# Attention and retention contractions of 16, 64 and 1 rows brought to 128 rows, and the chunk mask moved into maxima and exponentials

## What is computed

```python
q = (rms_norm(c_q, cq_g) @ w_uq).reshape(bn, lp, 16, 128 + 64)       # latent attention, 16 heads
s = einsum(q_nope, k_nope) + einsum(q_rope, k_rope)                  # k_rope is shared by all heads
mask = valid[None, :] & (cid[None, :] <= qcid[:, None])              # cid = position // 64
p = softmax(where(mask, s * MLA_SCALE, -1e30))
o_a = einsum('bhqk,bkhd->bqhd', p, v)
# retention, 8 heads of 256, chunkwise: scores * decay, times values, plus a carried state
s = einsum('bnhd,bmhd->bhnm', qc, kc) * intra
o_b = silu(g) * groupnorm(s @ vc + (qc @ state) * xi)
merged = sigmoid(ga) * (o_a @ w_pa) + sigmoid(gb) * (o_b @ w_pb)
h = layer_norm(ALPHA * h + merged @ w_out)
h = layer_norm(ALPHA * h + moe(h))                                   # 32 experts, top 2 of one group
```

## Time and profile before

| | |
|---|---|
| median of three runs | 2192.99 us (2190.24 to 2193.17) |
| profiled execution | 2191.38 us, of which the span from first to last instruction is 2189.6 us |
| PE busy | 2096.2 us, 96% |
| DVE busy | 1579.4 us, 72% |
| ACT busy | 1262.1 us, 58% |
| DMA, mean share of 16 engines | 40 to 60% until 1100 us, full from 1200 us |
| mean granted TensorE clock | 0.986 |

### The profile page before, as it was taken

The page is one execution under the profiler, slowest core; times in us unless marked ns, Lnnn a source line. Parts: engine busy times, 40 slices in busy tenths (PEclk is TensorE's granted clock), DMA queues, the critical chain, the costliest instruction groups (busy, mean ns, idle before and its releaser), DMA issues.

```text
span 2189.6 us, 30203 instructions
## 1 busy us (share of the span) xinstructions
PE 2096.2 (96%) x11524; PEld 1756.2 (80%) x11524; DVE 1579.4 (72%) x1373; ACT 1262.1 (58%) x1004; POOL 107.4 (5%) x78
## 2 busy tenths in 40 slices
PE   7999999999999999999999999999999999999991
PEld 6998777899999997887787778777877777777771
DVE  6645444453545455445668999999999999999996
ACT  5434433333232323333346888888888888888881
POOL 1000000000000000000000000000000000000000
PEclk9999999999999999999999999999999999999995
DMA  6554234655454544556865999999999999999993
GB/s 206 144 145 157 97 108 144 213 175 183 143 173 140 174 146 141 187 192 226 251 242 212 414 421 420 422 420 420 419 419 417 420 419 416 418 415 419 418 370 137
DMA packets 164615, 602.40 MB, mean 275 GB/s; under 512 B 20336, under 2 KB 28672, under 8 KB 113440
## 3 DMA queue, kind: packets, MB, share of 16 engines
q1 hardware_dynamic: 160800, 593.81, 71.5%
q0 software_dynamic: 3744, 7.59, 1.1%
HBM read 595.05 MB, written 18.89 MB: 280 GB/s over the span
## 4 chain that ended last, share of the span: by engine, by line
PE 69%; DVE 14%; DMA 7%; issue 7%; ACT 2%; POOL 0%; DVEq 0%; POOLq 0%; SPq 0%; ACTq 0%
PE ps L1720 20%; PE ps L1704 14%; DVE wl L667 11%; DMA raw<-in_w_dram 7%; PE ps L953 6%; PE ps L954 5%; PE ps L2075 4%; PE ps L950 3%; ACT wh L543 2%; PE ps L1825 2%; PE ps L1805 2%; PE ps L975 2%; PE ps L923 1%; PE ps L1792 1%; DVE yall L801 1%
## 5 line engine op out<-in xcount | busy, mean ns | idle before, releaser
L667 DVE TENSOR_TENSOR wl<-raw,wh 128x2048 fp32r<-128x2048 f32 x352 | 792.6, 2288 | 39.8 <-ACT wh L543 38.5
L543 ACT ACTIVATE wh<-raw 128x2048 fp32r<-128x2048 f32 x352 | 671.3, 1915 | 134.0 <-DMA raw<-in_w_dram 81.9
L1329 DVE TENSOR_TENSOR wl<-raw,wh 128x2048 fp32r<-128x2048 f32 (+1 forms) x169 | 382.1, 2264 | 290.1 <-ACT wh L1145 290.0
L1145 ACT ACTIVATE wh<-raw 128x2048 fp32r<-128x2048 f32 (+1 forms) x169 | 320.0, 1896 | 454.7 <-DMA raw<-in_w_in_dram 278.1
L953 PE MATMUL ps<-wh,xg 128*128 128x512 f32 x900 | 374.8, 416 | 21.4 <-DVE wl L667 21.3
L954 PE MATMUL ps<-wl,xg 128*128 128x512 f32 x900 | 352.9, 392 | 0.0
L1704 PE MATMUL ps<-hth,wh 128*128 128x272 f32 (+1 forms) x896 | 260.1, 290 | 3.2 <-DVE wl L1329 1.8
L1704 PE MATMUL ps<-htl,wh 128*128 128x272 f32 (+1 forms) x896 | 257.2, 287 | 0.0
L1704 PE MATMUL ps<-hth,wl 128*128 128x272 f32 (+1 forms) x896 | 256.9, 287 | 0.0
L953 PEld LDWEIGHTS ps<-wh,xg 128*128 128x128 f32 x900 | 169.8, 189 | 72.7 <-DVE wl L667 32.6
L953 PE MATMUL ps<-wh,hx 128*128 128x512 f32 x508 | 202.9, 399 | 4.2 <-DVE hx L794 4.2
(11 more groups left out here) (340 smaller groups left out, 3074.3 us busy)
## 6 DMA issues: line engine op xcount, KB each, us to landing
raw<-in_w_dram SPq DMA_DIRECT2D x384, 1024.0 KB, 10.3
raw<-in_w_in_dram SPq DMA_DIRECT2D x104, 1024.0 KB, 5.1
raw<-in_w_pa_dram SPq DMA_DIRECT2D x16, 1024.0 KB, 5.1
raw<-in_w_pb_dram SPq DMA_DIRECT2D x16, 1024.0 KB, 5.1
raw<-in_w_out_dram SPq DMA_DIRECT2D x16, 1024.0 KB, 5.2
raw<-in_w_ukv_dram SPq DMA_DIRECT2D x8, 1024.0 KB, 5.4
yrow<-yscr SPq DMA_DIRECT2D x4, 1024.0 KB, 8.1
raw<-in_w_uq_dram SPq DMA_DIRECT2D x8, 384.0 KB, 3.5
```

The source lines that it names most:

```text
L543: nc.scalar.activation(wh2[:, x % HELD, :], raw2[:, slot2(x), :], ACT.Copy).then_inc(s_wh2, 1)
L667: nc.vector.tensor_tensor(wl2[:, slot2(x), :], raw2[:, slot2(x), :], wh2[:, x % HELD, :].bitcast(F32), ALU.subtract).then_inc(s_wl2, 1)
L1145: nc.scalar.activation(wh[:, n % RING1, 0:c], raw1[:, n % RING1, 0:c], ACT.Copy).then_inc(s_wh, 1)
L1329: nc.vector.tensor_tensor(wl[:, n % RING1, 0:c], raw1[:, n % RING1, 0:c], wh[:, n % RING1, 0:c].bitcast(F32), ALU.subtract).then_inc(s_wl, 1)
```

## The change

Every small contraction now spans 128 rows:

- `vm`, `ptm`, `vnm` and `stm` are declared with 128 partitions. Their rows 16 to 127 are set to zero once and stay zero; the copies still write the first 16 rows.
- `kr` has two planes of 128 rows. Plane a holds the rotary key in the half of its rows that belongs to head a of a pair, and zeros in the other half. The product takes all 128 rows of the queries of both heads of the pair.
- The mask product is gone. The maxima and exponentials run over the keys that a half tile of 64 queries sees (`SEEN`: 80, 144, 208 and 272 keys): four instructions on 64 partitions in place of two on 128, on DVE and on ACT. The masked places of `prob` are set to zero once.
- The query latents are computed for 256 columns in place of 272, and the operations on them are narrower by as much.
- DVE zeroes `kr` after its setup copies and `ptm`, `prob` and `vm` after the `lo` of the next unit; `vnm` and `stm` are zeroed after the attention loop, with a semaphore `s_zero` on which ACT waits before retention.
- The table `rowmask`, its DMA and the two small ACT copies of it and of the ones are gone, and some constants lie elsewhere.

```diff
@@ -32,7 +32,7 @@
-LAT_BANK, SS_BANK = (0, 4), (6, 5)
+LAT_BANK, SS_BANK, LAT_C0 = (0, 4), (6, 5), (N_META, 0)
@@ -132,15 +132,17 @@
-        vm = place("vm", [N_META, H_MLA * VH], A0 + 17408)
+        vm = place("vm", [P, H_MLA * VH], A0 + 17408)
+        SEEN = [(t, slice(64 * c, 64 * (c + 1)), KT0 * t, KT0 * t + (KT0, KT1)[t] - 64 * (1 - c))
+                for t in range(TT) for c in range(2)]
-        ptm = place("ptm", [N_META, 2, SEQ], 199680)
+        ptm = place("ptm", [P, 2, SEQ], 199680)
-        vnm = place("vnm", [N_META, 2 * DK], R0 + 4096)
+        vnm = place("vnm", [P, 2 * DK], R0 + 4096)
-        stm = place("stm", [N_META, 2, SEQ], R0 + 9216)
+        stm = place("stm", [P, 2, SEQ], R0 + 9216)
-        kr = place("kr", [P, LT], K0 + 4736)
-        rowmask = place("rowmask", [1, P], K0 + 5824)
+        kr = place("kr", [P, 2, LT], K0 + 3712)
...
@@ -1184,10 +1186,10 @@
-                for t, (c0, c1) in enumerate(((0, KT0), (KT0, KT0 + KT1))):
-                    e = nc.scalar.activation(prob[:, h % 2, c0:c1], ps[:, 4 + h % 2, c0:c1], ACT.Exp,
-                                             bias=amax[:, h % 2, t:t + 1], scale=MLA_SCALE,
-                                             accum_out=asum[:, h % 2, t:t + 1])
+                for t, r, c0, c1 in SEEN:
+                    e = nc.scalar.activation(prob[r, h % 2, c0:c1], ps[r, 4 + h % 2, c0:c1], ACT.Exp,
+                                             bias=amax[r, h % 2, t:t + 1], scale=MLA_SCALE,
+                                             accum_out=asum[r, h % 2, t:t + 1])
...
@@ -1236,9 +1238,6 @@
-                if n == 2:
-                    nc.scalar.activation(rowmask_r[:, :], rowmask[:, :], ACT.Copy)
-                    nc.scalar.activation(ones_r[0:1, 0:64], ones[0:1, 0:64], ACT.Copy).then_inc(s_msk, 1)
@@ -1255,6 +1254,7 @@
+            act.wait_ge(s_zero, 1)
...
-                nc.vector.tensor_tensor(kr[:, :], krt[:, :], krt2[:, :], ALU.add).then_inc(s_kr, 1)
+                for a in range(2):
+                    r = slice(ROPE * a, ROPE * (a + 1))
+                    k = nc.vector.tensor_tensor(kr[r, a, :], krt[r, :], krt2[r, :], ALU.add)
+                k.then_inc(s_kr, 1)
...
-                nc.vector.tensor_reduce(amax[:, h % 2, 0:1], ps[:, 4 + h % 2, 0:KT0], AXX, ALU.max)
-                own.after(nc.vector.tensor_reduce(amax[:, h % 2, 1:2], ps[:, 4 + h % 2, KT0:KT0 + KT1], AXX, ALU.max))
+                for t, r, c0, c1 in SEEN:
+                    m = nc.vector.tensor_reduce(amax[r, h % 2, t:t + 1], ps[r, 4 + h % 2, c0:c1], AXX, ALU.max)
+                own.after(m)
...
+                    nc.vector.memset(kr[:, :, :], 0.0)
+                if n == 3:
+                    nc.vector.memset(ptm[:, :, :], 0.0)
+                    nc.vector.memset(prob[:, :, :], 0.0)
+                    own.after(nc.vector.memset(vm[:, :], 0.0))
...
+            nc.vector.memset(vnm[:, :], 0.0)
+            nc.vector.memset(stm[:, :, :], 0.0).then_inc(s_zero, 1)
...
             for u in range(4):
-                t_unit(N_CQ + u, 0, u, [(b, 0, True) for b in range(4)])
+                t_unit(N_CQ + u, 0, u, [(b, X0, True) for b in range(4)], c0=X0, width=SEQ)
...
@@ -1843,11 +1857,7 @@
-                    nc.tensor.matmul(o, qro[ROPE * a:ROPE * (a + 1), 2 * g, q], kr[ROPE * a:ROPE * (a + 1), 0:kt],
-                                     start=False, stop=False, skip_group_check=True)
-
-                    m = nc.tensor.matmul(ps[:, 4 + h % 2, c0 + kt - 64:c0 + kt], rowmask_r[:, :], ones_r[0:1, 0:64],
-                                         start=False, stop=True, skip_group_check=True)
+                    m = nc.tensor.matmul(o, qro[:, 2 * g, q], kr[:, a, 0:kt], start=False, stop=True, skip_group_check=True)
```

More of the change, by code:

```diff
@@ L168, in moe_trunk @@
         ones = place("ones", [P, P], K0 + 1024)
-        cos_b = place("cos_b", [P, LT], K0 + 2560)
-        sin_b = place("sin_b", [P, LT], K0 + 3648)
-        kr = place("kr", [P, LT], K0 + 4736)
-        rowmask = place("rowmask", [1, P], K0 + 5824)
-        rowmask_r = place("rowmask_r", [1, P], K0 + 5824, F32R)
-        ones_r = place("ones_r", [1, 64], 203904, F32R)
+        cos_b = place("cos_b", [P, LT], K0 + 1536)
+        sin_b = place("sin_b", [P, LT], K0 + 2624)
+        kr = place("kr", [P, 2, LT], K0 + 3712)
         lngb = place("lngb", [P, 2, KD], K0 + 6336)
@@ L200, in moe_trunk @@
         s_x = [sem(f"s_x{t}") for t in range(TT + 1)]
-        s_msk = sem("s_msk")
+        s_zero = sem("s_zero")
         s_raw = [sem(f"s_raw{i}") for i in range(RING1)]
@@ L1197, in transposed @@
                 nc.scalar.activation(pt[:, h % 2, :], ps[:, 4 + h % 2, 0:3 * P], ACT.Copy)
-                nc.scalar.activation(ptm[:, h % 2, :], ps[0:N_META, 6 + h % 2, SEQ:2 * SEQ],
+                nc.scalar.activation(ptm[0:N_META, h % 2, :], ps[0:N_META, 6 + h % 2, SEQ:2 * SEQ],
                                      ACT.Copy).then_inc(s_ptc, 1)
@@ L1264, in values @@
                 else:
-                    nc.scalar.activation(vnm[:, :], ps[0:N_META, 6, :], ACT.Copy).then_inc(s_vn, 1)
+                    nc.scalar.activation(vnm[0:N_META, :], ps[0:N_META, 6, :], ACT.Copy).then_inc(s_vn, 1)
             def ret_gate(g):
@@ L1379, in scale_latents @@
                 dve.wait_ge(s_sq, count)
-                own.after(nc.vector.reciprocal(crs[:, j, :], crs[:, j, :]))
+                c = LAT_C0[j]
+                own.after(nc.vector.reciprocal(crs[:, j, c:LT], crs[:, j, c:LT]))
                 for b in range(KR):
-                    nc.vector.scalar_tensor_tensor(csq[:, j, b, :], clat[:, j, b, :], cg[:, j, b:b + 1],
-                                                   crs[:, j, :], ALU.mult, ALU.mult).then_inc(s_cn, 1)
+                    nc.vector.scalar_tensor_tensor(csq[:, j, b, c:LT], clat[:, j, b, c:LT], cg[:, j, b:b + 1],
+                                                   crs[:, j, c:LT], ALU.mult, ALU.mult).then_inc(s_cn, 1)
             def latent_lo(j, count):
@@ L1524, in scores @@
                 else:
-                    nc.vector.tensor_tensor(stm[:, :, :], ps[0:N_META, 7, :].rearrange("p (a q) -> p a q", a=2),
+                    nc.vector.tensor_tensor(stm[0:N_META, :, :], ps[0:N_META, 7, :].rearrange("p (a q) -> p a q", a=2),
                                             decay_m[:, bass.ds(2 * g, 2), :], ALU.mult).then_inc(s_std, 1)
@@ L1745, in square_sums @@
                 for b in range(KR):
-                    m = nc.tensor.matmul(ps[:, SS_BANK[j], 0:LT], ones[:, :], csq[:, j, b, :],
+                    m = nc.tensor.matmul(ps[:, SS_BANK[j], LAT_C0[j]:LT], ones[:, :], csq[:, j, b, LAT_C0[j]:LT],
                                          start=b == 0, stop=b == KR - 1)
```

21 lines of the change are left out of this document (13 added, 8 removed).

## The result

The changed kernel takes 2162.92 us (median of four runs, 2160.03 to 2165.18), the kernel before beside it 2193.08 us (2190.24 to 2194.72). The ratio is 0.9863 with a 95% interval of 0.9846 to 0.988: 30 us faster. The forecast was 2158, within 2152 to 2168. The profiled execution of the changed kernel took 2163.33 us, its span is 2161.5 us, against 2189.6 us before. So the two traces to be compared differ by 28.1 us, and the forecast had 34.0.

The account below looks back on a forecast made before the run. PE was taken as the bound, busy 96%, so savings ahead of the experts move everything forward. Attention 26.1, retention 6.1, latents 1.5 and start 0.3 sum to 34.0 us, giving 2158 us; own range 2153 to 2163, 8-in-10 range 2152 to 2168.

Parts of the forecast that it names:

- two signs: Forecast wrong if L1859 to L1860 with 272 columns stays over 0.6 us, or PE waits for `prob`.
- price per change of rows: On PE in attention and `retain`: each change of contracted rows between neighbouring matmuls costs some 0.2 us, masks included.
- Retention: Eight calls of `retain` on PE: 0.76 us gained each, for four changes of rows, 6.1 us in all.
- the rival that swallows them: Retention: faster `retain` only lengthens PE's waits for low parts, the 6.1 us are lost, 2164 us; 6%.
- Query latents: 192 matmuls on PE go from 272 to 256 columns, gaining 1.5 us.
- Start: Kernel start: one constant DMA fewer on POOL lets PE begin sooner, gaining 0.3 us, between 0 and 0.6.
- The softmax chain "costs nothing": Attention steps: half-tile maxima and exponentials add 1.3 us, hidden by a cover of 0.8 to 1.4 us before PE asks.
- 26.1: Attention, 16 heads: 1.63 us gained per head on PE from eight changes of rows, 26.1 us in all.
- the softmax chain takes over: Attention: half-partition instructions exceed the 0.8 us cover, each excess paid per head; 1 us over gives 2174 us; 6%.
- The memsets: Zeroing of the padded buffers on DVE, 3.8 us at most for `ptm`, `prob` and `vm`, falls into idle time; costs nothing.
- Only the masks go: The 0.2 us gaps belong to fp32 products in general, so the gain is only 8.8 us, 2184 us; 5%.
- Bare weight loads: Loads hide only behind matmuls on other rows, so padded products expose theirs; 5 us slower, 2198 us; 2%.

Follow-up runs that it names:

- e1: Changed kernel with 128-row products kept, but the one-row mask products and the two full maxima and exponentials brought back; 2171.94 us, ratio 0.9902.
- e2: Changed kernel, masks still absent, but rotary, meta value and retention products contract 64, 16 and 16 rows again; 2185.62 us, ratio 0.9965.
- e5: Changed kernel with two full maxima and exponentials, and the mask again a product, but of 128 rows; 2162.71 us, ratio 0.9865.
- e9: Changed kernel with DVE's sum of `xh` and `xl` behind the experts held until POOL has issued the last scatter; 2162.0 us, ratio 0.9865.

## Why the prediction was right, and where it was off

**The number.** The measured 2162.92 us lies inside the stated range, at its upper part, and at the edge of the forecast's own 2153 to 2163. The mechanism that carried the sum held. One of the two signs by which the prediction called itself wrong did appear, a wait for `prob`, and 1.8 us were lost where it had not looked; that these stayed within the range is in part luck, and so are the 0.9 us that an earlier rise of the clock gave back.

**The bound and the price per change of rows.** PE was the bound, and what it saved ahead of the experts arrived: 29.9 us were still there at the last `yall`. A step came out at 8.58 us for 8.55 forecast. The gain per step without a wait is 1.60 us for 1.63. The price of some 0.2 us for each change was measured in four ways: 0.19 (e1), 0.20 (the six left in e2), 0.15 (e1 against e5), 0.19 (`retain`). The prediction put the masks themselves into it. Of the 1.60 us two masks' own time is 0.25 (e5), and 1.35 is left for eight changes, 0.17 each on the mean.

**Retention.** 6.1 us forecast, 6.1 measured, and its waits for low parts stayed at 1.8 us: the rival that swallows them is out.

**Query latents.** 1.5 us for 1.5: from the first product with 256 columns to the last, PE's instructions move from 0.5 to 2.0 us ahead of the kernel before. The narrower sums of squares (`csq`) give another 0.1.

**Start: not to be told from nothing.** Between the two traces the gain of 0.3 us became a loss of 0.4. PE's first instruction moved from 13.49 to 13.78, since the last constant table landed later although POOL issued it at 7.32 instead of 7.87. But in the traces of the other ten versions without the DMA of `rowmask` that instruction starts at 13.15 to 13.62, and in e1, which has it, at 13.36. The scatter is larger than the term, so neither the forecast's sign nor the loss is shown to belong to the edit. A DMA fewer in the queue was no measure of when the last one lands.

**The softmax chain "costs nothing": the step that failed.** Two things were off in it. The first is its size: I took 1.3 us, at most 1.9, and it is 1.8. Four maxima take 1.39 us for 0.69, and four exponentials with their accumulator reads 248.74 to 250.76, some 2.0 us for 1.0. A half-partition instruction cost what a full one of its columns costs (an exponential of 144 columns 0.38 us and one of 272 columns 0.48 us, on 64 partitions as on 128), which was the upper bound and should have been the value. Even so the cover of the ordinary step, 0.9 us, is in the forecast 0.8 to 1.4. The second is what decided: the cover was worked out from one ordinary step. The prediction said that DVE's start doesn't move. In every fourth step it does, since ACT has a table load and the sigmoid between the now longer exponentials and the cast for which DVE's `lo` waits, and the maxima stand behind the `lo`. The first step was not an ordinary one either: its cover was 2.0 us before, not 4.4. Steps with the sigmoid, and the first one, are 3 + 1 of 16. They cost 146.0 - 142.6 = 3.4 us, which is nearly all of the 3.9 us that attention fell short of 26.1. The rival "the softmax chain takes over" had the right mechanism; its price per head was paid in four of 16 heads.

**The memsets.** Hidden, as forecast. DVE at the start of the changed kernel, against the earlier trace rows:

```profile
47.54 1.76 DVE L1472 MEMSET vm<- 128x2048 f32 x1 [0.38 <-issue]
54.16 2.29 DVE L1329 TENSOR_TENSOR wl<-raw,wh 128x2048 fp32r<-128x2048 f32 x1 [4.85 <-ACT wh L1144]
```

The idle time ahead of that `lo` is shorter, 4.85 for 8.70 us, and nothing comes later for it.

**The other rivals.** Only the masks go (2184): out, e1 keeps the masks and gains 20.6 us. Bare weight loads (2198): out, by the load rows above and by e5, in which an additional product of 128 rows costs 0.12 us. The rule of the Trainium skill on which it stood, in "TensorE: Matmul & The Clock Gate", Part 3, isn't what these traces show: the load at 245.18 begins while a matmul on the same 128 rows runs, and it is the load on 64 rows that starts 0.36 us late. Another one fits, in "TensorEngine Tiling (Array Packing)", Key Properties: changing the tiling mode drains the engine. The rows of this study agree with it, at 0.08 to 0.20 us per change; that it is a drain is not seen in them, only that the next load starts late.

**The tail.** Not in the prediction at all. 1.8 us were lost there with DVE's pause ahead of its last sum; e9, which puts a wait in the pause's place, gets 1.1 of them back. Why the pause is gone is argued and not shown.

**The sum.** 34.0 - 28.1 = 5.9 us, in the two profiled executions: 3.9 in attention, 0.7 at the start, 0.5 between retention and the last expert (most of it at the fall of the clock described below), 1.8 in the tail, less 0.1 in the latents and 0.9 by an earlier rise of the clock. The medians differ by 30.2 us.

## What to carry to other kernels

Count the changes of the number of contracted rows between neighbouring matmuls, not the rows or the small matmuls: here one cost 0.15 to 0.20 us in most places, and two adjacent small products of different heights must both be filled up before the last changes go. Before a cost is put down as hidden, look at its cover in the worst step of the loop, the one in which another engine's queue has something more, and not in a typical one, and in the first step too. At the end of this kernel a pause of 1.4 us on DVE, which no line of the program asks for, went with a tail that is 1.8 us shorter; look at the last instructions of both traces even where nothing was edited.

## What the runs showed of the hardware that I had not expected

- Products of 96 and 112 contracted rows behave as ones of 128, and those of 32 and 64 as those of 16: 2.42 against 3.19 us, a difference of 0.77, where 16 against 128 rows made 0.78.
- The scatter on POOL takes 0.89 us with DVE idle and 3.46 us beside DVE's sum of two SBUF operands. It ends 0.7 us after the first of the two instructions of that sum (2123.53 + 3.46 = 2126.99, against 2122.73 + 3.52 = 2126.25). The other 31 scatters take about 2.25 us, the first of them beside a `lo` that ends 0.9 us ahead of it (1188.02 + 2.27 = 1190.29, against 1187.13 + 2.25 = 1189.38). So it looks as if a scatter waits for the DVE instruction beside it and then takes about what it takes alone; no run tests this.
- At the start PE's matmuls of 272 columns go from a spacing of 0.23 to one of 0.125 us at a time that differs between the traces: 24.45 us in the kernel before, 22.83 in the changed one, 21.89 to 24.66 in all. By spacing that is the step from 1.2 to 2.4 GHz, yet the profile's granted clock (the 1.00 in these two windows on PE of the kernel before) reads full on both sides of it, with 11 records in 2 us and with 17. That a part of the 3 to 5 us between runs of one kernel is this is likely, and not shown, since each kernel has one trace.

```profile
22.00:24.00 2.00, 2.00 (x11) 1.00 0.01 4
24.00:26.00 2.00, 2.00 (x17) 1.00 0.00 0
```

- After PE's wait of 2.7 us for `mrg` the granted clock fell in the changed kernel and didn't in the kernel before, with the same wait. The stretch of the 32 transposes took 5.1 us for 3.9, of which half was lost, since PE's next wait was shorter. Windows on PE of the changed kernel (stretch, length, busy us, clock, DMA share, GB/s), and then of the kernel before:

```profile
1006.00:1008.00 2.00, 2.00 (x12) 0.50 1.06 400
```

```profile
1037.00:1040.00 3.00, 3.00 (x25) 1.00 1.08 382
```

  A clock of 0.50 is the level of 1.2 GHz. Twelve records stand in 2 us there, and 25 in 3 us at the full clock. Of the thirteen traces only the kernel before and e1 have no fall there, and e1, with the same code there as the changed kernel, took 3.9 us at 1.00. Why it fell in the others is open.
